# Splitting streamed weights in quarter blocks on GpSimd, in a two-block fp32 transformer kernel

## What is computed

```python
h = rms_norm(x, norm_mix);  proj = h @ w_in                     # block 1
y_a = pool_mixer(u_pool, w_pool) * pool_scale                   # trailing means over 2, 4, 8, 16 tokens
y_b = stick_breaking_attention(q, k, v)                         # 8 heads of 64
x = x + (sigmoid(g_a) * (y_a @ w_branch_a) + sigmoid(g_b) * (y_b @ w_branch_b)) @ w_out
x = x + (silu(h @ w_ffn_gate) * (h @ w_ffn_up)) @ w_ffn_down    # h = rms_norm(x), hidden 2816
x = x + sigmoid(rms_norm(x) @ w_ple_gate) * (p @ w_ple_proj)
x = rms_norm(x, norm_final)
u = rmsnorm(x, g_pre);  proj = u @ w_in_2                       # block 2
y_a = rwkv7_branch(...);  y_b = mla_branch(...)
out = x + rmsnorm((g_a * y_a + g_b * y_b) @ w_o, g_post)
```

## Time and profile before

| | us |
|---|---|
| median of 3 runs (2819.19 to 2821.75) | 2819.62 |
| the profiled execution | 2824.97 |
| its span, first to last instruction | 2823.1 |
| TensorE busy | 2699.1 |
| TensorE weight loads busy | 2115.2 |
| VectorE busy | 1341.4 |
| GpSimd busy | 935.8 |
| ScalarE busy | 684.6 |

### The profile page before, as it was taken

The page is one execution under the profiler, slowest core; times in us unless marked ns, Lnnn a source line. Parts: engine busy times, 40 slices in busy tenths (PEclk is TensorE's granted clock), DMA queues, the critical chain, the costliest instruction groups (busy, mean ns, idle before and its releaser), DMA issues.

```text
span 2823.1 us, 50266 instructions
## 1 busy us (share of the span) xinstructions
PE 2699.1 (96%) x21508; PEld 2115.2 (75%) x21508; DVE 1341.4 (48%) x1291; ACT 684.6 (24%) x964; POOL 935.8 (33%) x414
## 2 busy tenths in 40 slices
PE   7999999999999999999999989998999999998987
PEld 6677778888888888888888756666677777776765
DVE  7844452214522122212366754343656565544588
ACT  3333340001211000000033334443131312112231
POOL 4322114444444344434444311113111221223466
PEclk9999999999999999999999999999999999999998
DMA  3100001112111111111122200001111110113443
GB/s 128 38 31 30 22 15 52 45 52 105 45 52 45 52 45 52 45 52 45 52 75 79 85 23 16 15 15 62 39 37 43 35 52 32 50 43 128 118 151 110
DMA packets 40749, 156.15 MB, mean 55 GB/s; under 512 B 4640, under 2 KB 5152, under 8 KB 39200
## 3 DMA queue, kind: packets, MB, share of 16 engines
q1 hardware_dynamic: 31392, 110.21, 12.1%
q10 hardware_dynamic: 9216, 43.78, 4.2%
HBM read 133.00 MB, written 20.97 MB: 55 GB/s over the span
## 4 chain that ended last, share of the span: by engine, by line
PE 85%; DVE 8%; issue 3%; ACT 3%; DMA 1%; POOL 1%; ACTq 0%; DVEq 0%; POOLq 0%; SPq 0%
PE dps L287 51%; PE dps L304 14%; PE aps L1684 6%; PE aps L1310 3%; PE aps L598 2%; PE dps L618 2%; PE dps L1323 1%; PE dps L609 1%; DVE h_lo L347 1%; PE dps L1331 1%; ACT mla_pt L1446 1%; DVE x_res L2528 1%; DVE sumsq L377 1%; PE aps L1587 1%; PE aps L1843 1%
## 5 line engine op out<-in xcount | busy, mean ns | idle before, releaser
L2601 POOL TENSOR_TENSOR w_hi<-w_raw,one 128x1024 fp32r<-128x1024 f32 x199 | 388.9, 1954 | 1843.1 <-PE dps L287 1323.3
L287 PE MATMUL dps<-h_hi,w_hi 128*128 128x512 f32 x1712 | 545.4, 395 | 25.2 <-POOL w_lo L2610 9.5
L287 PE MATMUL dps<-h_lo,w_hi 128*128 128x512 f32 x1712 | 539.5, 391 | 0.0
L287 PE MATMUL dps<-h_hi,w_lo 128*128 128x512 f32 x1712 | 539.2, 391 | 0.0
L2603 POOL TENSOR_TENSOR w_lo<-w_raw,w_hi 128x1024 fp32r<-128x1024 f32 x199 | 525.4, 2640 | 15.6
L287 PEld LDWEIGHTS dps<-h_hi,w_hi 128*128 128x128 f32 x1712 | 322.0, 189 | 100.6 <-issue 14.1
L287 PEld LDWEIGHTS dps<-h_hi,w_lo 128*128 128x128 f32 x1712 | 323.2, 189 | 68.1
L287 PEld LDWEIGHTS dps<-h_lo,w_hi 128*128 128x128 f32 x1712 | 323.3, 189 | 67.7 <-issue 0.2
L304 PE MATMUL dps<-h_hi,w_hi 128*128 128x512 f32 x528 | 181.5, 416 | 5.8 <-ACT rw_b L2140 2.5
L304 PE MATMUL dps<-h_lo,w_hi 128*128 128x512 f32 x528 | 178.1, 406 | 4.1 <-DVE rw_xm L2036 3.3
L304 PE MATMUL dps<-h_hi,w_lo 128*128 128x512 f32 x528 | 174.3, 408 | 1.2 <-DVE rw_akt L2052 1.1
(11 more groups left out here) (371 smaller groups left out, 4025.8 us busy)
## 6 DMA issues: line engine op xcount, KB each, us to landing
w_raw<-w_stream SPq DMA_DIRECT2D x200, 512.0 KB, 3.5
x_again<-x_t ACTq DMA_DIRECT2D x2, 4096.0 KB, 13.4
gates<-gate_out ACTq DMA_DIRECT2D x16, 512.0 KB, 2.7
tmp<-gates ACTq DMA_DIRECT2D x15, 512.0 KB, 4.1
x_t<-x_res ACTq DMA_DIRECT2D x4, 1024.0 KB, 3.9
out_t<-x_again SPq DMA_DIRECT2D x16, 256.0 KB, 2.0
back<-branches ACTq DMA_DIRECT2D x7, 512.0 KB, 8.2
x_res<-x_t ACTq DMA_DIRECT2D x2, 1536.0 KB, 12.0
```

The costliest lines, as they stand in the source:

```text
L287: mm = k.nc.tensor.matmul(k.dps[0:rows, pair, h * HALF:(h + 1) * HALF], w[:, slot, sub + t, 0:rows], x(t)[:, h * HALF:(h + 1) * HALF], sta ...
L2601: g.tensor_tensor(k.w_hi[:, s], k.w_raw[:, s], ones, ALU.mult).then_inc(k.sem("w_hi_done"), 1)
```

## The change

GpSimd makes a block's split in pieces. Up to block 177 a piece is a quarter of a block (two tiles, 256 elements a partition): first the four high pieces, one after the other, then the four low pieces, each of which waits until its high piece is counted in `w_hi_done`. In the first block the order is two high, two low, `w_split`, and the same again. From block 178 on a block is one piece, that is `w_hi` and `w_lo` as before. `w_split` still counts up once a block (twice in the first), after the last low piece. The counts that the low pieces wait for are adapted. Nothing else changes: SP, TensorE, ScalarE and VectorE run the same code.

```diff
+PIECES = 4
+
+
 def stream_pool(k, pool, n_blk):
 
     g = k.nc.gpsimd
     g.memset(k.one[:, :], 1.0).then_inc(k.sem("one_done"), 1)
     pool.wait_ge(k.sem("one_done"), 1)
-    ones = k.one[:, 0:1].to_broadcast([P, SUB * P]).rearrange("p (a b) -> p a b", a=SUB)
-
-    def split(i, s, first):
+
+    def piece(n, pieces):
+        return slice(SUB // pieces * n, SUB // pieces * (n + 1))
+
+    def high(s, n, pieces):
+        size = SUB // pieces
+        ones = k.one[:, 0:1].to_broadcast([P, size * P]).rearrange("p (a b) -> p a b", a=size)
+        at = piece(n, pieces)
+        g.tensor_tensor(k.w_hi[:, s, at], k.w_raw[:, s, at], ones, ALU.mult).then_inc(k.sem("w_hi_done"), 1)
+
+    def low(s, n, pieces, count):
+        at = piece(n, pieces)
+        pool.wait_ge(k.sem("w_hi_done"), count)
+        return g.tensor_tensor(k.w_lo[:, s, at], k.w_raw[:, s, at], k.w_hi[:, s, at].bitcast(F32), ALU.subtract)
+
+    def split(i, s, first, pieces, highs):
         pool.wait_ge(k.sem(f"w_loaded{s}"), i * 16 + 16)
         if not first:
             pool.wait_ge(k.sem("blk_done"), i * 2 + (s - 1))
-        g.tensor_tensor(k.w_hi[:, s], k.w_raw[:, s], ones, ALU.mult).then_inc(k.sem("w_hi_done"), 1)
-        pool.wait_ge(k.sem("w_hi_done"), i * 2 + (s + 2))
-        g.tensor_tensor(k.w_lo[:, s], k.w_raw[:, s], k.w_hi[:, s].bitcast(F32), ALU.subtract).then_inc(k.sem("w_split"), 1)
+        for n in range(pieces):
+            high(s, n, pieces)
+        for n in range(pieces):
+            done = low(s, n, pieces, i * (2 * pieces) + (highs + s * pieces + n + 1))
+        done.then_inc(k.sem("w_split"), 1)
 
     pool.wait_ge(k.sem("w_loaded0"), 16)
-    for n in range(2):
-        part = slice(4 * n, 4 * n + 4)
-        g.tensor_tensor(k.w_hi[:, 0, part], k.w_raw[:, 0, part], ones[:, part], ALU.mult).then_inc(k.sem("w_hi_done"), 1)
-        pool.wait_ge(k.sem("w_hi_done"), n + 1)
-        g.tensor_tensor(k.w_lo[:, 0, part], k.w_raw[:, 0, part], k.w_hi[:, 0, part].bitcast(F32), ALU.subtract).then_inc(k.sem("w_split"), 1)
-    split(0, 1, True)
+    for half in range(2):
+        for n in (2 * half, 2 * half + 1):
+            high(0, n, PIECES)
+        for n in (2 * half, 2 * half + 1):
+            done = low(0, n, PIECES, n + 1)
+        done.then_inc(k.sem("w_split"), 1)
+    split(0, 1, True, PIECES, 0)
 
     stop = BLK["merge2"] // 2 + 1
     with pool.Fori(1, stop) as i:
         for s in range(2):
-            split(i, s, False)
+            split(i, s, False, PIECES, 0)
     back_pool(k, pool)
     with pool.Fori(stop, n_blk // 2) as i:
         for s in range(2):
-            split(i, s, False)
+            split(i, s, False, 1, stop * (2 * PIECES - 2))
```

## The result

The median fell from 2820.68 us (2819.19 to 2822.08) to 2798.75 us (2797.24 to 2800.49), a ratio of 0.9925 with an interval of 0.9914 to 0.9937. The profiled execution took 2800.49 us with a span of 2798.7 (before: 2824.97 and 2823.1), mean granted clock 0.991 (0.985).

What follows compares the result with a forecast made beforehand. TensorE, busy 96%, was taken as the bound, with some waits behind VectorE operations held up by GpSimd splits. Stalls 7.6 us plus clock 3.4 less losses 3.6 gave 7.4 us, a median of 2812.2 us; range 2802 to 2825.

Steps and rivals of the forecast that it cites:

- Rival D: The four high pieces keep the port as one instruction would; DVE still waits up to 1.9 us; 2819 us, chance 12%.
- The sign named for it: If right, no DVE operation before 2590 us would be over its kind by more than 0.6 us.
- Rival A: Stalls shrink as forecast but the clock gives nothing: 4.0 us gained, 2815.6 us, chance 25%.
- Rival C: Pieces wait for whole DVE operations; ten to twelve blocks come 1 to 1.5 us late: 2826 us, chance 13%.
- What the clock gives: Half-speed time coming back: 1.5 us at 2037 us, 1.2 at 1630, 0.7 at 110, nothing at 40; sum 3.4 us.
- Rival B: Everything comes back: stalls 7.6 us, clock 10.7 us, half the losses, 1.8 us; 16.5 us gained, 2803 us, chance 15%.
- What DVE gets back: Shorter holds shrink stalls at six places, 7.6 us in all; at 2037 us from 3.28 to about 1.1, 2.0 taken.
- The start: Stalls shrink by 1.2 us at 40 us (eight additions, less what h_lo loses), 0.8 at 101 and 0.8 at 110.
- What DVE loses: Pieces falling between dependent operations delay DVE: 0.8 us for h_lo before 1590 us, 1.0 in attention pairs; 3.6 with other losses.
- The latent projections: At 1628 us the 1.81 us wait behind trig and pe_raw goes, latent_sq's stays at 2 us; 1.8 us taken.
- The merge: Before the second merge, block 177's quarters move GpSimd's queue and PE's waits back: loss 1.5 us (0.5 to 2.5).
- Attention pairs: In pairs 1 to 3, five holds of 0.35 us each replace one loss of 2 us: 1.0 us lost in all.

Runs made afterwards that it cites:

- eighths: Single tiles, sixteen instructions a block, up to block 177 in place of the changed kernel's quarters: 2822.9 us, ratio 1.0004.
- all4: The changed kernel with quarters to the end, through the second merge and out2 as well: 2820.09 us, ratio 0.9997.
- shift_c: The changed kernel with GpSimd repeating w_hi, 7.2 us of extra work, ahead of the split of block 80 in the FFN: 2805.62 us.

## Why the prediction was wrong

**Right.** The bound, the mechanism and its places. The pieces: 0.58 and 0.71 us foreseen, 0.58 and 0.70 measured (a block 5.1 us, not 5.7: the gaps between pieces don't show). Half block of wd_ad: slack 0.40 us left, no loss. Rival D fell by the lines of the earlier trace rows's answer: both `tensor_scalar` ran beside high pieces and lost 0.3 to 0.4 us each. The sign named for it came true but for the instructions beside `back_pool`: measured against the shortest instruction of the same line, tiles and shape in either profile, 78 VectorE instructions before 2590 us were over their kind by more than 0.6 us in the kernel before, and 7 are now, four of them beside `back_pool`, whose subtractions aren't split, and the other three over by 0.60 to 0.61. Rival A is out: the clock gave back 12.6 us. Rival C didn't come up to block 177; `eighths`, with smaller pieces, and `all4`, behind block 177, show it real.

**Wrong.** The direction and the places were right; two parts of the sum were too small, by factors of 3.7 and 3. "What the clock gives" was put at 3.4 us, and the clock cost 12.6 us less; the stalls, 7.6 less 3.6 us of losses, were put at 4.0 us net, and TensorE's idle time fell by 12.0. Term by term, against the table above:

- "What the clock gives", 3.4 us. I took about a half or less of what each low stretch costs as coming back. Behind 2037 us, where I took 1.5 us, all of 3.4 came back in both profiles. At 40 us I took nothing, for a stall of over 2 us was to stay; 1.16 us stayed and nothing was lost behind it. This is the step that failed most. Over two profiles each, the clock cost 37.4 us before (41.6, 33.2) and 24.8 after (24.8, 24.8): 12.6 us. By stage, on the mean, 6.8 us of it are at the start, 0.9 in the latent projections, 2.6 in MLA, 3.4 in RWKV's start and 1.6 behind; the attention pairs 1 to 3 lost 2.6. Of these MLA's are placement, and the start's 6.8 are the mean of 10.2 and 3.4. Rival B, 2803 us, was the nearest, and 15% was too little for it, but it came near in part by luck: 6 of its 10.7 us for the clock stood at 40 and 110 us, priced from that one execution, and its stalls and losses made 5.8 us net where 12.0 went.
- "What DVE gets back" at 2037 us: 1.1 us of stall should stay, 0.27 did (3.0 us less in the place of 2.0). The two instructions lost 0.3 to 0.4 us each, not a hold of 0.5.
- The start: 12.5 us for the eight sums (0.34 us over 1.22 each) where my holds gave 13.3, and `h_lo` ahead of them, which I booked as a loser, went from 10.5 to 9.5 us. PE's idle time until 127 us fell by 4.5 us, not by 2.8.
- "What DVE loses", `h_lo` before 1590 us: I took 0.8 us of loss. The five waits of 0.7 to 1.7 us, 4.98 us, became three, 4.04. The sign was wrong.
- The latent projections: the wait for `latent_sq`, which was to stay at 2 us, fell to 1.10; the chain of six gained 1 us. The `pe_raw` term was right.
- The merge: 0.6 us of loss, not 1.5. The first wait grew by 1.5 us, to 4.45, but the second stayed at 5.08, not 6.5: VectorE's chain hides it. Attention pairs: 1.8, not 1.0, most of it the low stretch at 345 us behind the wait of 1.63 us, which took the place of 1.07 and 0.43.
- MLA: no term at all, 2.4 us, from where the low stretches fell and not from the splits beside it.

Idle time, the mean of two profiles each, fell from 125.0 to 113.0 us. It and the clock's 12.6 us add up to 24.6, where the spans differ by 22.5: the two parts overlap a little, where the clock is low while PE idles.

The base was also read as firmer than it is. I took stretches of the earlier trace rows as properties of the kernel; 10.2 us of them before 130 us were that execution's, against 1.7 to 3.4 in three others. Setting the forecast 5.3 us down to the median made that good for the result, but the terms at 40 and 110 us were priced from it. In MLA, whether the first wait of 1.77 us has a low stretch with it goes with where the low stretch before it started (the table behind `shift_c`). What stays open is what decides that start, and why some of these stretches repeat in each execution of a kernel and others don't.

## What to carry to other kernels

Where GpSimd's and VectorE's instructions keep each other waiting, cut GpSimd's as short as its slack allows, and no shorter: read the slack by stage (eighths gained 4.4 us beside the attention pairs and lost more than that where VectorE is dense; quarters in out2 cost 17.5 us). Price a stall of TensorE of 2 us or more with the slow stretch that can follow it (1.7 to 2.8 us more than the stall, where one did), and take it all back when the stall goes. And before a difference of 2 or 3 us is put down to an edit, profile each kernel more than once and look, stage by stage, whether the low stretches fell in the same places: here the same difference came between executions of one kernel and between kernels that are alike in that stage.

## What was not expected of the hardware

- One and the same code up to 130 us lost 10.2, 3.4, 1.7 and 1.7 us to the low clock in four executions with the same stalls of 3.3 and 4.0 us.
- A wait of 1.77 us in MLA, equal to 0.01 us in all kernels, was followed by half speed in some and not in others; it went with a difference of 1 us in where the low stretch before it started.
- Beside a dense chain of VectorE operations that take 1.2 us alone, eight pieces of 0.42 us took 10.25 us. A w_hi of 1.89 us behind eight subtractions of 0.61 us was again kept out for the whole chain, as in the earlier trace rows:

```profile
2684.90 6.02 POOL L2606 TENSOR_TENSOR w_hi<-w_raw,one 128x1024 fp32r<-128x1024 f32 x1 [5.91 <-PE dps L2444]
```

That is a row of the changed kernel's second profile. The Trainium skill's section named above has the other engine wait until the instruction that holds the pair ends, which would be one subtraction; this row doesn't agree.
